# Forgetting attention: the copies of the second parts move from ScalarE to VectorE

## The reference

```python
def forgetting_attention(q, k, v, log_f):
    cum = jnp.cumsum(log_f.astype(F32), axis=1).transpose(0, 2, 1)
    def block(i):                       # 128 queries
        s = jnp.einsum('bqhd,bkhd->bhqk', qb, k, preferred_element_type=F32) * scale
        s = s + (cq[..., :, None] - cum[..., None, :])
        s = jnp.where(kpos[None, :] <= qpos[:, None], s, -jnp.inf)
        p = jax.nn.softmax(s, axis=-1)
        return jnp.einsum('bhqk,bkhd->bqhd', p.astype(v.dtype), v)
```

## Time and profile before

| | us |
|---|---|
| Median of 3 runs | 2835.12 (2835.11 to 2835.93) |
| The profiled execution | 2835.61 |
| Its span (first to last instruction) | 2833.8 |
| PE busy in the span | 2600.8 (92%) |
| DVE busy | 1357.4 (48%) |
| ACT busy | 1033.0 (36%) |
| POOL busy | 383.7 (14%) |

### The profile page before, as it was taken

The page is one execution under the profiler, slowest core; times in us unless marked ns, Lnnn a source line. Parts: engine busy times, 40 slices in busy tenths (PEclk is TensorE's granted clock), DMA queues, the critical chain, the costliest instruction groups (busy, mean ns, idle before and its releaser), DMA issues. The chain is left out here.

```text
span 2833.8 us, 31714 instructions
## 1 busy us (share of the span) xinstructions
PE 2600.8 (92%) x12428; PEld 2168.8 (77%) x12428; DVE 1357.4 (48%) x2308; ACT 1033.0 (36%) x1515; POOL 383.7 (14%) x283
## 2 busy tenths in 40 slices
PE   4889988879799999999999798888799999999998
PEld 3668767779787888888887676777688888888877
DVE  4568769865443323232447623444433333333366
ACT  4342135556432222222336411555432222222254
POOL 1112122301011222221000030111102222220000
PEclk8999988889899999999999899778899999999999
DMA  4101000000231111111437420000421111113365
GB/s 128 31 23 45 23 23 23 16 1 2 75 119 60 46 51 47 51 48 42 140 100 250 147 62 0 1 1 1 164 72 52 48 52 46 52 45 112 97 233 176
DMA packets 163344, 191.50 MB, mean 68 GB/s; under 512 B 11156, under 2 KB 132340, under 8 KB 163196
## 3 DMA queue, kind: packets, MB, share of 16 engines
q1 hardware_dynamic: 157888, 171.46, 19.2%
q10 hardware_dynamic: 5308, 18.01, 1.6%
HBM read 172.64 MB, written 16.81 MB: 67 GB/s over the span
## 5 line engine op out<-in xcount | busy, mean ns | idle before, releaser
L128 PE MATMUL l_ps<-rest_hi,l_whi 128*128 128x512 f32 x1408 | 439.6, 390 | 4.7 <-DVE rest_lo L1842 4.7
L128 PE MATMUL l_ps<-rest_hi,l_wlo 128*128 128x512 f32 x1408 | 439.5, 390 | 0.0
L128 PE MATMUL l_ps<-rest_lo,l_whi 128*128 128x512 f32 x1408 | 439.2, 389 | 0.0
L1709 POOL TENSOR_TENSOR l_wlo<-l_raw,l_whi 128x1024 fp32r<-128x1024 f32 x88 | 213.0, 2421 | 982.2 <-ACT l_whi L1628 982.2
L128 PEld LDWEIGHTS l_ps<-rest_hi,l_whi 128*128 128x128 f32 x1408 | 264.7, 188 | 60.2 <-DVE rest_lo L1842 5.2
L128 PEld LDWEIGHTS l_ps<-rest_lo,l_whi 128*128 128x128 f32 x1408 | 264.7, 188 | 54.8
L128 PEld LDWEIGHTS l_ps<-rest_hi,l_wlo 128*128 128x128 f32 x1408 | 264.5, 188 | 55.0
L1848 DVE SCALAR_TENSOR_TENSOR l_y_v<-l_ps,main_conv,l_y_v 128x1023 f32<-128x1023 f32 x44 | 56.4, 1282 | 337.7 <-ACT l_y_v L1662 337.7
L1628 ACT ACTIVATE l_whi<-l_raw 128x1024 fp32r<-128x1024 f32 x156 | 164.2, 1053 | 127.3 <-PE l_ps L128 119.3
L1662 ACT ACTIVATE l_y_g<-l_ps,main_conv 128x1024 f32<-128x1024 f32 x44 | 53.1, 1207 | 382.2 <-PE l_ps L128 382.2
L1848 DVE SCALAR_TENSOR_TENSOR l_y_g<-l_ps,main_conv,l_y_g 128x1023 f32<-128x1023 f32 x44 | 56.4, 1283 | 282.8 <-ACT l_y_g L1662 282.8
(11 more groups left out here) (302 smaller groups left out, 4964.4 us busy)
## 6 DMA issues: line engine op xcount, KB each, us to landing
l_raw<-in_ffn_w_in SPq DMA_DIRECT2D x88, 512.0 KB, 3.8
l_raw<-in_ffn_w_out SPq DMA_DIRECT2D x68, 512.0 KB, 3.6
l_rawl<-in_ffn_w_out SPq DMA_DIRECT2D x44, 512.0 KB, 4.2
front_raw<-in_even_w_in SPq DMA_DIRECT2D x20, 512.0 KB, 3.6
l_rawe<-in_ffn_w_out SPq DMA_DIRECT2D x20, 512.0 KB, 3.5
ofront_raw<-in_odd_w_qkv SPq DMA_DIRECT2D x10, 512.0 KB, 4.0
setup_xin<-in_x SPq DMA_DIRECT2D x8, 512.0 KB, 11.1
fox_negc<-negc_dram SPq DMA_DIRECT2D x8, 512.0 KB, 3.5
```

The source lines that it names most:

```text
L128: mm = pe.matmul(o, w, m, start=a, stop=z)
L1709: pool.tensor_tensor(wlo[u % 3][:], raw_up[u % 2][:], whi[u % 3][:].bitcast(F32), ALU.subtract).then_inc(up_lo, 1)
```

## The change

One line. With forgetting, the second part of a step (c > 0) is now in `by_dve`, as it was without forgetting already:

```diff
@@ -1156,7 +1156,7 @@
     last = [j - 1 for j in first[1:]] + [NPARTS - 1]
     RING, AHEAD, EXP_AHEAD, NP, ROWS, GRP = 3, 5, 3, 6, 8, 4
     HEADS = len(heads)
-    by_dve = [not forget and c > 0 for n, c, e in parts]
+    by_dve = [c > 0 for n, c, e in parts]
     dve_upto = [sum(by_dve[:j + 1]) for j in range(NPARTS)]
```

## The result

The changed kernel takes 2866.03 us (median; 2862.7 to 2869.75), the kernel before 2835.11 beside it (2833.06 to 2835.93). The ratio is 1.0111 with a 95% interval of 1.0093 to 1.0128: slower by 1.1%, some 31 us. The forecast was 2855 with a range of 2844 to 2863: the direction was right, the size too small, and the result lies 3 us above the range. Its stage is also the shortest of two profiles of this kernel, which bears on the numbers further down.

A forecast was written before the change was run, and what follows sets the result against it. DVE was taken to set the end of the forgetting-attention stage. Copies 11.9, tail 0.7, old blocks -3.3, new blocks 7.4 and new waits 3.0 gave 19.7 us on 2835.1: forecast 2855, range 2844 to 2863.

The forecast's parts named there:

- What DVE gets in addition shows in the total, unless it falls into idle or blocked time: Forgetting-attention stage: DVE sets its end, busy 190.0 of 215 us, with 11.5 us idle up to its last selection work.
- The copies: Forgetting-attention stage: 32 copies move from ACT to DVE, 15.6 us, less overlap and the last three: 11.9 us on the path.
- The new blocks: Turns behind heads 0 and 3: L816 and L818 now meet POOL's subtractions, 5.6 us lost each, net 7.4 for both.
- Rival B: Same two turns: L814, L816, L818 slip through or only one turn is caught; 2847 to 2851 us, chance 0.25.
- of it the idle time behind each packing is absorbed, 1.9 us: Turns behind heads 0 and 3: DVE's idle behind each packing takes up 1.9 of 5.6 us lost, net 3.7 each.
- The old blocks: Heads 1, 4 and 5, where POOL already blocked DVE: two copies become free and POOL ends earlier, giving back 3.3 us.
- New waits: Forgetting-attention stage: PE's lead over DVE shrinks to one part at 32 places, so DVE waits for scores: +3 us, bounds -7.7 and 10.4.
- While PE has its full clock DVE does not wait now: Read from 553 to 582 us in the kernel before: clock 1.00, DVE busy 28.5 of 29 us.
- Rival C: Forgetting-attention stage: PE's clock stays low, DVE's waits reach 10.4 us, triples lose 9.6; 2864 us, chance 0.15 including what lies between.
- a PE that has to catch up gets its full clock back: Forgetting-attention stage: reason for not taking PE as the bound, though busy 175.9 of 215 us at clock 0.83.
- The tail: End of the forgetting-attention stage: part 7's last copy stands behind DVE's last selection work, so the sums start 0.7 us later.
- Everything after it shifted by the same amount: Stages behind forgetting attention: they start about 20 us later and keep their lengths; a changed length would show the prediction wrong.

The follow-up runs named there:

- a_again: The changed kernel without any edit, profiled a second time (also called the repetition): 2867.0 us, ratio 1.0111 to the kernel before.
- a_early: Changed kernel with two selection decisions drawn forward, so L814, L816, L818 precede the 256-wide copy in the turns from heads 0 and 3: 2861.0 us, ratio 1.0083.
- a_back4: Changed kernel with DVE copying part j behind the maximum of part j+4 instead of j+5: 2855.6 us, ratio 1.0066 to the kernel before.
- b_norm: Kernel before, with the product of the division (L1350) moved from DVE to ACT as four scaled copies of 64 columns: 2831.6 us, ratio 0.9984.
- a_only7: Changed kernel, but only the 256-wide copy of part 7 of each head moves to DVE, 8 copies: 2850.6 us, ratio 1.0050 to the kernel before.
- padded kernels: Kernel before with 9, 18 or 21 sums added at the end of DVE's forgetting-attention work: end +6.5, +23.0, +33.0 us; changed kernel with 2 or 5: +32.9, +37.0.
- a_small: Changed kernel with POOL's three subtractions for heads 2 to 7 cut from 1024 to 8 columns, work left out: 2853.8 us, ratio 1.0065.

## Why the prediction was right in its sign and too small

Two steps failed. The first is the sentence "What DVE gets in addition shows in the total, unless it falls into idle or blocked time", with the terms for idle time that hang on it: together -0.8 us in the sum, +5.3 measured. The second is that everything behind the stage would only be shifted: it grew by 4.4 us, 4.2 in the repetition. A later stage that changes its length was one of the prediction's own signs of being wrong.

**The copies: held, 1.3 us too small.** Predicted 11.9, measured 13.2 (29 copies of 13.9 us in the segments, less 0.7 of overlap). The durations were right; the overlap of 0.07 us that I took off at each was the one between the two instructions of the earlier trace rows; what the segments leave for it is 0.7 in all.

**The new blocks: the place exact, the amount and the net too large.** L814 was predicted 0.05 us ahead of POOL and came 0.08 and 0.09 ahead; L816 and L818 waited out one POOL instruction each, 4.2 us per turn, where I had taken 5.6 as the mean of two patterns (the second, with L814 caught as well, did not occur). Rival B fell. But the step "of it the idle time behind each packing is absorbed, 1.9 us" had the wrong size: idle in segments 1 and 4 went from 3.3 to 4.3 (2.9 in the repetition), so little or nothing was absorbed. And measured by taking the blocks away, they were worth about 6 us or less (a_early) and not 7.4. With the old blocks taken off, the forecast of 4.1 us agrees with the 4 to 5 that the two kernels without POOL's long subtractions show.

In the earlier trace rows L816 was due 0.02 us ahead of POOL's instruction and waited it out. The rule of the Trainium skill that I weighed ("SBUF — State Buffer", Who interferes with whom: who issues first holds the pair) lost to the trace again: it leaves one POOL instruction waited out per turn, and in both turns two were, L816 behind the first and L818 behind the second. L818 starts at 419.85 and POOL's second subtraction at 419.86, in the later turn at 508.41 and 508.43:

```profile
419.86 2.35 POOL L1210 TENSOR_TENSOR fox_k_lo<-even_fqk,fox_k_hi 64x1024 fp32r<-64x1024 f32 x1
```

The starts lie 0.02 us apart, so this speaks against the rule only as far as the trace's starts tell who issued first.

**The old blocks: held.** They gave back 2.9 us where I had 3.3.

**New waits: direction right, size wrong. This is the main miss in the stage.** With the absorption and the new waits together I had idle fall by 0.8 (+3.0 - 3.8); it rose by 5.3. The mechanism was named in the prediction (the copy stands behind the maximum of part j+5, PE's lead shrinks to one part), but priced as an extra of 3 us beside the copies. a_back4 shows what it is worth: about 12 us. The sentence that it rested on, "While PE has its full clock DVE does not wait now", was read from one stretch: of the 12 waits for scores in the kernel before, 5 lie where the clock was 1.00, 3.9 us in all (1.56 of them at 551.43, just ahead of that stretch). The sentence quoted above treats DVE as a resource whose work can be added and taken away. The runs show a loop of DVE's maximum, the copy, PE's sums and PE's next scores: take 6 us from DVE and give ACT 20 (b_norm), and the stage's mark moves 0.3; add 3.4 in one bad place (a_only7) and it costs 14.8, 8.4 of them at most by its two blocks.

**The clock: a rival, half right.** Rival C said that the same work of PE, spread over a longer time, costs clock, and gave 2864. Of its three parts one came: the clock fell from 0.83 to 0.75 and PE was busy 18.3 us longer. The waits did not come to 10.4 and the triples did not lose 9.6, so its number was near the result for a sum that was wrong in its parts. I had argued against it from one stretch at clock 1.00. PE's 6.5 us of idle there were four waits for ACT's copies, the very thing that the change moves. And I had set PE aside with "a PE that has to catch up gets its full clock back": in the tail PE had everything left to catch up and was busy 8.6 of 9.6 us at clock 0.57, in a_again 10.2 of 11.3 at 0.50.

**The tail: too small, and hidden by luck.** Predicted +0.7, measured -1.2 in the first profile and +1.7 in the repetition (11.4 against 9.6 and 9.7). I had looked at who starts it and not at PE's clock in it, which was 0.57 before, and 0.79 and 0.50 in the two profiles of the changed kernel.

**"Everything after it shifted by the same amount": failed, +4.4 us** (+4.2 in the repetition). The padded kernels show that such a shift can itself be worth -4 to +3.5.

Summed up as it was written: copies +1.3 against the forecast, new blocks gross -2.8, old blocks +0.4, idle +6.1, tail -1.9, together +3.1 in the stage (19.7 to 22.7, with rounding); then +4.4 behind it; and 3.8 because the changed kernel's profiled execution was 3.3 us below its median, and the other's 0.5 above. Of those 3.3 the tail of that one profile may be the greater part: in the repetition it was 2.9 us longer.

## What to carry to other kernels

Before moving a step to the busiest engine, write down not only its length but its place in that engine's order, and who stands waiting for it there: here the place was worth about 12 us and the length 13. Where two engines wait for each other in a ring, the idle time of neither is a reserve; price an edit in it by the lead that it leaves the other engine, and expect removed stalls to come back as waits at about half of their size (40% in the changed kernel, 55% in the one before). And put an uncertainty of several us on the unchanged stages behind an edit: here the same stages, only started later, took from 4.1 us less to 3.5 more. Before a single profile is read to 1 us, look for a stretch whose length goes with the granted clock: here the tail, 8.4 or 11.4 us in two profiles of one kernel.

## What was new about the hardware

Of small DVE instructions in a row, each waited out a POOL subtraction of its own: L816, 0.23 us of work, took 2.25 to 2.28 in these turns, and L818 behind it 2.38 to 2.40, each about the length of one POOL instruction (4.8 us for two). Nor does POOL always go first. In the kernel before, the scan L838 waited from 552.04 until POOL's second subtraction ended at 553.88 and then ran until 554.97 (it takes 1.22 us unhindered, in a_small), and POOL's third took 3.17 us instead of 2.36:

```profile
553.96 3.17 POOL L147 TENSOR_TENSOR fox_q<-even_fqk,fox_q 64x1024 fp32r<-64x1024 f32 x1
```

So the two took turns: a DVE instruction that waited ran when the POOL instruction ended, and the next one of DVE's waited for the next of POOL's. The copies from PSUM were never stretched: in the changed kernel a copy of 384 columns at 451.34, in the middle of POOL's subtractions that began at 449.34, took its usual time (all eight of this width took 0.55 to 0.56):

```profile
451.34 0.56 DVE L1341 COPY fox_probT<-fox_TR 128x384 f32<-128x384 f32 x1
```

The granted clock over the first 5.5 us of the turn was 0.69 in the kernel before and 1.00 in the same kernel with that stage started 10.6 us later. And in the tail of the stage a clock of 0.50 lasted although PE was busy for 10.2 of 11.3 us (a_again).
